# Where modulation tiles, weight splits and start-up transfers stand in a two-block transformer kernel

## The chip, the core and the metric

The kernel runs on one core of a Trainium2 chip. The metric is device microseconds (us) of one execution. The core has a matrix engine (TensorE, called PE in the profile; its weight loads are PEld), a vector engine (DVE), a scalar engine (ACT), GpSimd (POOL), and SyncE (SP), which issues DMAs. SBUF is on-chip memory of 128 partitions; PSUM holds eight banks that PE writes.

## What is computed

Two stacks of depth 2 run one after the other on 256 tokens of width 1024, in fp32. The first has an input projection, three kinds of sequence mixing (a gated recurrence, sparse attention with compressed, selected and windowed keys, and a forgetting attention), an output projection and a squared-ReLU feed-forward. The second is modulated by a condition `c` and carries a second sequence `ctx` of 256 tokens through most of its first layer:

```python
for layer in range(2):
    h = rmsnorm(x, norm1_g[layer]);  proj = h @ w_in[layer]
    mix = concat(hgrn2(...), nsa(...), fox(...))
    x = x + mix @ w_o[layer]
    x = x + square(relu(rmsnorm(x, norm2_g[layer]) @ w_up[layer])) @ w_down[layer]
for l in range(2):
    mod  = silu(c) @ w_ada[l] + b_ada[l]          # 9 vectors of 1024: shifts, scales, gates
    modc = silu(c_ctx) @ w_ada[l] + b_ada[l]
    h  = h  + 0.5 * gt1 * swiglu(ada_norm(h, g_ffn1[l], sh1, sc1), ...)
    ...                                           # conv, latent attention, Fourier branches
    h  = h  + 0.5 * gt3 * swiglu(ada_norm(h, g_ffn2[l], sh3, sc3), ...)
out = rms_norm(h, g_final)
```

## The kernel before

**Weights stream through one ring.** `ring` has 4 slots of 128 x 1024 fp32 (512 KB). SP walks a fixed list of chunks in order (`stream_plan`, `segments`); chunk number n goes into slot n modulo 4, and SP waits until the chunk that lay there has been released (`used[slot]`) before it issues the load. Since SP issues in order, a slot that is released late holds up all loads behind it.

**Split products.** A precise fp32 product is made of three fast ones. For each weight chunk ACT copies the ring slot into `w_hi` (a rounded copy, L733), DVE subtracts it into `w_lo` (L761), both with two buffers, and PE runs the low pass (L802) and then pairs of high passes (L809, L812). ACT may write a `w_hi` only once PE has begun the chunk before, which says that the buffer's old chunk is finished. `splits_ahead` puts the splits of a group's later chunks, and of the next group's first, at the group's start on ACT and DVE; `first_split` does the first chunk of a product.

**The feed-forward of the second block.** `ffn1` and `ffn2` are 22 groups of two chunks (256 or 512 columns; 512 in layer 0, and in layer 1 for `ffn1`). `ffn1_out` and `ffn2_out` are 8 groups of three chunks (8, 8 and 6 tiles of 128). After each of these groups DVE adds the gated result to the residual (L2040) and accumulates squares for the next norm (L1700, L1702), in `gated_add`.

**Where the modulation is computed.** The two layers' modulation is 144 row tiles of 512 KB. 84 of them are done by PE in block 1, as `ada` chunks between its other work: `ADA_TICKS` says how many chunks start at each of 28 points ("ticks") of a layer, ticks 0 to 3 before the attention and ticks 4 to 27 one in each turn of the attention's loop, which runs 22 units through PE, DVE and ACT. `ada_pe` (L883) is this work; a batch of 28 chunks ends with a copy on ACT (L894), 8 small matmuls (L871) and bias adds on DVE (L904). The other 60 are done by DVE in layer 0 of block 2, for layer 1: such a tile comes through the ring as one more chunk of a group, and `row_dot` makes two weighted sums of it (L915 and L917) and releases the slot. `ffn1` and `ffn2` carry one row tile a group; `ffn1_out` carries two a group, taken by `row_pair` at the group's end; `ffn2_out` carries none.

**End of the attention.** ACT copies the last head outputs (L1199), rounds the mixed heads to `hn_hi` (L1390, three parts), DVE makes `hn_lo` (L1395), and then the out-projection `wo` begins with its first split (L733 and L761).

**Start.** ACT issues both halves of `x` (L2578, L2579) and three constant and parameter transfers, then waits for `x`, issues two more (L2585, L2586), waits for the parameters and computes silu of the condition (L2589). PE waits for that before its first matmuls, the mean square (L980). SP issues the first two weight chunks at once.

## Time and profile before

| | us |
|---|---|
| median of 3 runs | 3090.91 (3089.37 to 3092.67) |
| the profiled execution's own time | 3086.55 |
| its span, first to last instruction | 3084.8 |
| PE busy | 2898.1, 94% |
| DVE busy | 1657.1, 54% |
| ACT busy | 1116.2, 36% |
| mean granted clock, share of full | 0.978 |

1.75 us of the profiled execution lie outside the span. Groups of rows further down come from one execution: "idle before" is the time in which an engine waited, with the work that ended the wait behind the arrow; a chain row says what the execution's end was waiting for at that time. "PEclk" is the granted TensorE clock, 1.0 being full.

### The profile page before, as it was taken

What the parts mean: (1) busy time and instruction counts of PE and PEld (TensorE: products, weight loads), DVE (VectorE), ACT (ScalarE), POOL (GpSimd) and SP (SyncE); (2) the same over time, 40 slices, a digit from 0 to 9 for tenths busy, and PEclk for the clock granted to TensorE, in tenths of its full rate; (3) what the DMA queues carried; (4) which work ended last, traced back from release to release, by engine and by line L of the source; (5) the groups of instructions that cost most, each with busy time, mean ns of one, the idle gap of its engine ahead of it and who ended that gap; (6) DMA issues with size and microseconds to landing.
All of it is one profiled execution on the core that took longest, in us unless ns stands there. A gap on an engine that the chain in (4) does not pass through costs nothing.

```text
span 3084.8 us, 45320 instructions
## 1 busy us (share of the span) xinstructions
PE 2898.1 (94%) x16648; PEld 2392.7 (78%) x16648; DVE 1657.1 (54%) x2831; ACT 1116.2 (36%) x1695; POOL 45.8 (1%) x36
## 2 busy tenths in 40 slices
PE   7898998899999998889999999999999998999998
PEld 6658998559988886666566678888788887688998
DVE  6446656346556664469334466653433336645665
ACT  4334535245442221133455232221322223385443
POOL 0100000000000000011000000000000000000000
PEclk9999999899999999999999999999999998999999
DMA  5464554555543443331222224442222223234454
GB/s 185 154 236 151 177 180 135 186 202 194 170 157 132 148 147 117 118 101 38 78 69 62 80 89 146 143 142 94 89 98 95 92 96 100 73 113 142 160 180 144
DMA packets 120091, 401.99 MB, mean 130 GB/s; under 512 B 13088, under 2 KB 22688, under 8 KB 119584
## 3 DMA queue, kind: packets, MB, share of 16 engines
q1 hardware_dynamic: 116320, 392.74, 38.5%
q10 hardware_dynamic: 3648, 7.59, 0.7%
q8 instruction: 79, 1.29, 0.2%
q14 instruction: 44, 0.36, 0.0%
HBM read 399.24 MB, written 1.05 MB: 130 GB/s over the span
## 4 chain that ended last, share of the span: by engine, by line
PE 81%; DVE 10%; DMA 3%; ACT 3%; DVEq 2%; issue 1%; SPq 0%; ACTq 0%
PE bank L802 21%; PE bank L812 21%; PE bank L809 21%; PE bank L2194 4%; DMA ring<-weights 3%; DVE hid L2447 2%; DVE w_lo L761 2%; PE bank L1484 2%; PE bank L883 1%; ACT w_hi L733 1%; PE bank L1942 1%; PE bank L1922 1%; PE bank L2280 1%; DVEq L2453 1%; DVE work L2011 1%
## 5 line engine op out<-in xcount | busy, mean ns | idle before, releaser
L761 DVE TENSOR_TENSOR w_lo<-ring,w_hi 128x1024 fp32r<-128x1024 f32 (+1 forms) x538 | 650.4, 1209 | 915.1 <-ACT w_hi L733 912.3
L733 ACT ACTIVATE w_hi<-ring 128x1024 fp32r<-128x1024 f32 (+1 forms) x538 | 562.9, 1046 | 1388.4 <-PE bank L802 1217.4
L809 PE MATMUL bank<-hn_hi,w_hi 128*128 128x256 f32 (+1 forms) x2816 | 888.3, 335 | 0.0
L812 PE MATMUL bank<-hn_lo,w_hi 128*128 128x256 f32 (+1 forms) x2816 | 887.9, 335 | 0.0
L802 PE MATMUL bank<-hn_hi,w_lo 128*128 128x256 f32 (+1 forms) x2816 | 559.9, 341 | 31.3 <-DVE w_lo L761 20.8
L809 PEld LDWEIGHTS bank<-hn_hi,w_hi 128*128 128x128 f32 x2816 | 539.3, 191 | 52.3
L812 PEld LDWEIGHTS bank<-hn_lo,w_hi 128*128 128x128 f32 x2816 | 539.1, 191 | 52.1
L802 PEld LDWEIGHTS bank<-hn_hi,w_lo 128*128 128x128 f32 x2816 | 444.8, 191 | 101.7 <-issue 45.2
L809 PE MATMUL bank<-hid_hi,w_hi 128*128 128x512 f32 (+1 forms) x704 | 250.3, 365 | 0.0
L812 PE MATMUL bank<-hid_lo_a,w_hi 128*128 128x512 f32 (+1 forms) x640 | 227.2, 364 | 0.0
L802 PE MATMUL bank<-hid_hi,w_lo 128*128 128x512 f32 (+1 forms) x704 | 166.9, 379 | 33.1 <-DVE w_lo L761 28.3
L802 PEld LDWEIGHTS bank<-hid_hi,w_lo 128*128 128x128 f32 x704 | 124.9, 195 | 63.0 <-DVE w_lo L761 35.6
L809 PEld LDWEIGHTS bank<-hid_hi,w_hi 128*128 128x128 f32 x704 | 134.3, 191 | 21.5
L812 PEld LDWEIGHTS bank<-hid_lo_a,w_hi 128*128 128x128 f32 x640 | 121.8, 190 | 19.3
L809 PE MATMUL bank<-up_hi,w_hi 128*128 128x256 f32 x512 | 125.6, 283 | 0.0
L812 PE MATMUL bank<-up_lo,w_hi 128*128 128x256 f32 x512 | 125.6, 283 | 0.0
L2194 PE MATMUL bank<-hid,ring 128*128 128x512 f32 (+1 forms) x352 | 124.2, 494 | 1.3 <-ACT hid L1986 1.3
L2447 DVE SCALAR_TENSOR_TENSOR hid<-work,par,hid 128x512 f32<-128x512 f32 (+1 forms) x180 | 117.4, 707 | 4.6
L812 PEld LDWEIGHTS bank<-up_lo,w_hi 128*128 128x128 f32 x512 | 98.3, 192 | 0.0
L809 PEld LDWEIGHTS bank<-up_hi,w_hi 128*128 128x128 f32 x512 | 98.3, 192 | 0.0
L2194 PEld LDWEIGHTS bank<-hid,ring 128*128 128x128 f32 x352 | 63.8, 189 | 42.7 <-issue 38.8
L1423 PE MATMUL bank<-hn_hi,w_lo 128*128 128x256 f32 (+1 forms) x160 | 58.2, 381 | 28.7 <-ACT hn_hi L971 20.2
(311 smaller groups left out, 3052.7 us busy)
## 6 DMA issues: line engine op xcount, KB each, us to landing
ring<-weights SPq DMA_DIRECT2D x692, 512.0 KB, 3.4
ring<-weights SPq DMA_DIRECT2D x32, 384.0 KB, 3.0
ring<-weights SPq DMA_DIRECT2D x32, 256.0 KB, 2.6
ring<-weights SPq DMA_DIRECT2D x32, 192.0 KB, 2.3
con<-consts ACTq DMA_DIRECT2D x1, 2063.0 KB, 9.1
ring<-weights SPq DMA_DIRECT2D x16, 128.0 KB, 2.1
con<-consts ACTq DMA_DIRECT2D x1, 1088.0 KB, 5.1
res<-x_cm ACTq DMA_DIRECT2D x2, 512.0 KB, 7.7
```

The lines of the kernel that those rows point to most:

```text
L733: act.activation(w_hi[:, even, 0:w], ring[:, slot, 0:w], ACT.Copy).then_inc(s.w_hi, 1)
L761: eng.tensor_tensor(w_lo[:, even, 0:w], ring[:, slot, 0:w], w_hi[:, even, 0:w].bitcast(F32), ALU.subtract).then_inc(s.w_lo, 1)
L802: mm = pe.matmul(dst, w_lo[:, number % 2, k * P:(k + 1) * P], x_hi(k), start=(start and k == order[0]), stop=False)
L809: pe.matmul(dst, high, x_hi(k), start=False, stop=False)
L812: mm = pe.matmul(dst, high, x_lo(k), start=False, stop=(stop and k == order[-1]))
L883: mm = pe.matmul(ada_bank(h)[rows, :], cs[:, k, COND_AT - 2 * q:COND_W - 2 * q], ring[:, slot, i * 4 * P:(i + 1) * 4 * P], start=(q == 0 a ...
L1423: mm = pe.matmul(dst[c], w_lo[:, even[c], k * P:(k + 1) * P], hn_hi[:, k, 0:w], start=(k == 0), stop=False)
L1484: mm = pe.matmul(bank[2 * parity(lin, g)][:, q], sq[:, k, q], ring[:, slot_of(lin, g, 0), k * P:(k + 1) * P], start=(k == 0), stop=(k == K ...
L1922: mm = pe.matmul(scores(x)[:, j * x.keys:(j + 1) * x.keys], q2[0:QK, x.h + j, x.tt * P:(x.tt + 1) * P], k2[0:QK, x.h + j, x.key0:x.key0 + ...
L1942: mm = pe.matmul(bank[7][rows, 0:P], v2[:, x.key0 // P + k, h * DH:(h + 1) * DH], pt[:, x.u % 2, (j * kt + k) * P:(j * kt + k + 1) * P], s ...
L2194: mm = pe.matmul(bank[2 * parity(lin, g)][:, 0:w], ring[:, slot_of(lin, g, 0), k * P:(k + 1) * P], src[:, k, 0:w], start=(k == 0), stop=(k ...
L2447: last = dve.scalar_tensor_tensor(out=dst, in0=src, scalar=taps[:, m, k:k + 1], in1=dst, op0=ALU.mult, op1=ALU.add)
```

## The change

- `ffn1_out` and `ffn2_out` of layer 0 carry **one** row tile a group each, instead of two and none. DVE takes it between the low parts of the group (`split_and_row`), not at its end. A group of either is now four chunks. The last gates' bias and factor 0.5 move to a small `row_gate` in layer 1.
- `ADA_TICKS` becomes a table for each layer: six ticks of two chunks, then ticks of four; 40 chunks in layer 0 and 44 in layer 1, where both had 42. Batches are 20, 20, 24 and 20 chunks instead of three of 28.
- `wo`'s first split moves on ACT from behind the attention into its turn 21, and on DVE ahead of the two last `mix_low`.
- At the start SP issues the first half of `x` ahead of the weights, whose first chunk waits until it has landed; ACT issues four transfers and the two large ones only after the first norm; PE waits for one constant set alone; silu of the condition is made later from a sigmoid (ACT) and a product (DVE).

```diff
-ADA_TICKS = [2, 2, 2, 4, 4, 0, 4, 0, 0, 4, 0, 0, 4, 0, 0, 4, 0, 0, 4, 0, 0, 4, 0, 0, 4, 0, 0, 0]
+ADA_TICKS = ([2, 2, 2, 2, 2, 2, 0, 4, 0, 0, 4, 0, 0, 4, 0, 4, 0, 4, 0, 4, 0, 4, 0, 0, 0, 0, 0, 0],
+             [2, 2, 2, 2, 2, 2, 0, 4, 0, 0, 4, 0, 0, 4, 0, 4, 0, 4, 0, 4, 0, 4, 0, 4, 0, 0, 0, 0])
-ADA_BATCH = 7
+ADA_QUADS = (5, 5, 6, 5)
...
-        order += [("ffn1", l, FF2, (8, 8) + rows, (0, 1)), ("ffn1_out", l, 8, (8, 8, 6) + 2 * rows, (0, 1, 2)),
+        order += [("ffn1", l, FF2, (8, 8) + rows, (0, 1)), ("ffn1_out", l, 8, (8, 8, 6) + rows, (0, 1, 2)),
...
-                  ("ffn2_out", l, 8, (8, 8, 6), (0, 1, 2))]
+                  ("ffn2_out", l, 8, (8, 8, 6) + rows, (0, 1, 2))]
...
                 if n >= 2:
                     unit_out(act, units[n - 2])
                 ada_act(act, l, TICK_ATT + n)
+                if n == len(units) - 1:
+                    first_split(split_high, act, PLAN["wo", l])
...
             mix_high(act, l, 2)
-            first_split(split_high, act, PLAN["wo", l])
...
             attention_dve(dve, l, units_block1(l))
+            first_split(split_low, dve, PLAN["wo", l])
             mix_low(dve, l, 1)
             mix_low(dve, l, 2)
-            first_split(split_low, dve, PLAN["wo", l])
...
             for g in turns(dve, lin, tail=2):
-                split_following(dve, lin, g, following)
+                if lin.cpg > lin.own:
+                    split_and_row(dve, l, which, lin, g, following)
+                else:
+                    split_following(dve, lin, g, following)
                 wait_products(dve, lin, g)
...
-                row_pair(dve, l, lin, g)
...
+        def split_and_row(dve, l, which, lin, g, following):
+
+            at = ROWS_AT["ffn1_out" if which == 0 else "ffn2_out"]
+            to = mods[:, 1, 2 * at:2 * (at + KT)].rearrange("p (m c) -> p m c", c=2)
+            split_ahead(split_low, dve, lin, g, 1, following)
+            row_dot(dve, lin, g, 3, to[:, g.m, :])
+            for j in (2, 3):
+                split_ahead(split_low, dve, lin, g, j, following)
...
+            if which == 0 and l == 1:
+                row_gate(dve, l)
...
             norm_act(act, 2 * l, PLAN["in_t", l], PLAN["down", l - 1] if l else None)
             if l == 0:
+                act.dma_start(con12[:, 0:CONST_SETS[1][1]], consts[1]).then_inc(s.consts1, 16)
+                act.dma_start(res[:, :, T:2 * T], ctx_cm).then_inc(s.ctx_in, 16)
...
         @block.sync
         def _(sp):
+            sp.dma_start(res[:, 0:KT // 2, 0:T], x_cm[:, 0:KT // 2, :]).then_inc(s.x_in, 16)
...
+                        if isinstance(chunk, int) and chunk == 0:
+                            sp.wait_ge(s.x_in, 16)
...
         @block.tensor
         def _(pe):
-            pe.wait_ge(s.consts, 48)
-            pe.wait_ge(s.csilu, 1)
+            pe.wait_ge(s.con0_in, 16)
...
         @block.scalar
         def _(act):
-            act.dma_start(res[:, 0:KT // 2, 0:T], x_cm[:, 0:KT // 2, :]).then_inc(s.x_in, 16)
             act.dma_start(res[:, KT // 2:KT, 0:T], x_cm[:, KT // 2:KT, :]).then_inc(s.x_in2, 16)
-            act.dma_start(con0[:, :], consts[0]).then_inc(s.consts, 16)
+            act.dma_start(con0[:, :], consts[0]).then_inc(s.con0_in, 16)
+            act.dma_start(par12[:, 0:PARAM_SETS[1][1]], params[1]).then_inc(s.consts, 16)
             act.dma_start(par0[:, :], params[0]).then_inc(s.consts, 16)
```

DVE's queue in the first groups of `ffn1_out`, layer 0, before. L761 makes a low part, L915 and L917 are one row tile, L2040, L1700 and L1702 are the gated add and the squares:

```order
L761 TENSOR_TENSOR w_lo<-ring,w_hi 128x1024 [waits w_hi]
L761 TENSOR_TENSOR w_lo<-ring,w_hi 128x768 [waits w_hi]
L761 TENSOR_TENSOR w_lo<-ring,w_hi 128x1024 [waits w_hi]
L2040 SCALAR_TENSOR_TENSOR res<-bank,mods,res 128x256 [waits used2]
L2040 SCALAR_TENSOR_TENSOR res<-bank,mods,res 128x256
L1700 TENSOR_TENSOR work<-res 128x512
L1702 TENSOR_TENSOR work<-work 128x512
L915 SCALAR_TENSOR_TENSOR conds,mods<-ring,con_65 128x1024 [waits landed3]
L917 SCALAR_TENSOR_TENSOR ring,mods<-ring,con_65 128x1024
L915 SCALAR_TENSOR_TENSOR conds,mods<-ring,con_65 128x1024 [waits landed0]
L917 SCALAR_TENSOR_TENSOR ring,mods<-ring,con_65 128x1024
L761 TENSOR_TENSOR w_lo<-ring,w_hi 128x1024 [waits w_hi]
```

The same engine and product after the change (the seventh group; the loop that runs the first six has the same order; L765 is L761, L923 and L925 are L915 and L917, L2071 is L2040):

```order
L765 TENSOR_TENSOR w_lo<-ring,w_hi 128x1024 [waits w_hi]
L923 SCALAR_TENSOR_TENSOR conds,mods<-ring,con_65 128x1024 [waits landed3]
L925 SCALAR_TENSOR_TENSOR ring,mods<-ring,con_65 128x1024
L765 TENSOR_TENSOR w_lo<-ring,w_hi 128x768 [waits w_hi]
L765 TENSOR_TENSOR w_lo<-ring,w_hi 128x1024 [waits w_hi]
L2071 SCALAR_TENSOR_TENSOR res<-bank,mods,res 128x256 [waits used2]
L2071 SCALAR_TENSOR_TENSOR res<-bank,mods,res 128x256
L1729 TENSOR_TENSOR work<-res 128x512
L1731 TENSOR_TENSOR work<-work 128x512
L765 TENSOR_TENSOR w_lo<-ring,w_hi 128x1024 [waits w_hi]
```

Four row instructions between the squares and the next low part have become two behind that low part. The group's row tile is always in slot 3 now.

ACT's queue at the end of the attention of layer 0, after the change (L737 is L733, L1209 copies a unit's transposed weights, L1216 is L1199, L1416 is L1390):

```order
L1216 ACTIVATE work<-bank 128x128 [waits att_v]
L737 ACTIVATE w_hi<-ring 128x1024 [waits lo_used,landed1]
L1209 ACTIVATE work<-bank 128x512 [waits att_v,att_t]
L1216 ACTIVATE work<-bank 128x128 [waits att_v]
L1416 ACTIVATE hn_hi<-work 128x4x256 [waits att_o]
L1216 ACTIVATE work<-bank 128x128 [waits att_v]
L1416 ACTIVATE hn_hi<-work 128x2x256 [waits att_o]
L737 ACTIVATE w_hi<-ring 128x1024 [waits lo_used,landed2]
```

The first `L737` stood between the last `L1416` and the second `L737` before. On DVE the low part of the same chunk has moved ahead of the two `hn_lo` subtractions in the same way.

## Rows read from the trace of the kernel before

**Rows 1.** The page: busy time of each engine, and the chain's shares.
```profile
PE 2898.1 (94%) x16648; PEld 2392.7 (78%) x16648; DVE 1657.1 (54%) x2831; ACT 1116.2 (36%) x1695; POOL 45.8 (1%) x36
...
PE 81%; DVE 10%; DMA 3%; ACT 3%; DVEq 2%; issue 1%; SPq 0%; ACTq 0%
```

**Rows 2.** `ffn1_out`, `ffn2_out`: length; PE, PEld, DVE, ACT, POOL busy; clock; DMA share.
```profile
1165.03:1335.57 170.54, 136.13 (x536) 106.15 (x537) 85.76 (x128) 28.65 (x33) 1.53 (x1) 0.93 0.37 123
2072.77:2198.00 125.23, 122.20 (x537) 100.37 (x537) 49.30 (x70) 28.85 (x33) 0.00 (x0) 1.00 0.32 101
```

**Rows 3.** Chain of waits in `ffn1_out`, layer 0: start, length, what.
```profile
1176.39 3.33 DMA ring<-weights
...
1180.83 1.22 DVE w_lo L761
...
1184.50 1.23 DVE conds L915
1185.73 1.14 DVE ring L917 x2
1186.97 1.23 DVE conds L915 x2
1188.20 1.15 DVE ring L917 x2
1189.35 1.15 DVE w_lo L761
```

**Rows 4.** DVE in one group of `ffn2_out`, layer 0: start, length.
```profile
2088.03 0.88 DVE L2040 SCALAR_TENSOR_TENSOR res<-bank,mods,res 128x256 f32<-128x256 f32 x2 [1.48 <-PE bank L812]
...
2090.37 1.22 DVE L761 TENSOR_TENSOR w_lo<-ring,w_hi 128x1024 fp32r<-128x1024 f32 x1
2094.63 0.96 DVE L761 TENSOR_TENSOR w_lo<-ring,w_hi 128x768 fp32r<-128x768 f32 x1 [3.04 <-ACT w_hi L733]
2100.29 1.23 DVE L761 TENSOR_TENSOR w_lo<-ring,w_hi 128x1024 fp32r<-128x1024 f32 x1 [4.70 <-ACT w_hi L733]
```

**Rows 5.** Stretches: `ffn1` with a row tile a group (layer 0), without (layer 1).
```profile
920.84:1165.03 244.19, 241.83 (x1057) 199.10 (x1057) 153.02 (x224) 64.80 (x81) 0.00 (x0) 0.99 0.40 138
2198.00:2442.15 244.15, 241.62 (x1056) 199.02 (x1057) 100.77 (x136) 62.99 (x80) 0.00 (x0) 0.99 0.28 92
```

**Rows 6.** The start on DVE and PE, in order of time.
```profile
7.33 1.43 DVE L2613 TENSOR_TENSOR work<-res 128x256 f32<-128x256 f32 x4 [4.66 <-DMA res<-x_cm]
10.12 1.43 DVE L2613 TENSOR_TENSOR work<-res 128x256 f32<-128x256 f32 x4 [1.36 <-DMA res<-x_cm]
...
12.87 5.48 PE L980 MATMUL bank<-work,con 128*128 128x256 f32 x16 [12.87 <-ACT conds L2589]
...
20.46 0.36 PE L1423 MATMUL bank<-hn_hi,w_lo 128*128 128x256 f32 x1 [2.11 <-ACT hn_hi L964]
```

**Rows 7.** PE: first two products of `wo`, layer 0; first, layer 1.
```profile
243.11 2.05 PE L802 MATMUL bank<-hn_hi,w_lo 128*128 128x256 f32 x8 [3.28 <-issue]
248.37 1.23 PE L802 MATMUL bank<-hn_hi,w_lo 128*128 128x256 f32 x8
...
688.82 2.05 PE L802 MATMUL bank<-hn_hi,w_lo 128*128 128x256 f32 x8 [3.28 <-issue]
```

**Rows 8.** Modulation chunks on PE around the start of layer 0's attention.
```profile
154.72 3.68 PE L883 MATMUL bank<-ring,conds 128*32 128x512 f32 x12 [0.54 <-DMA ring<-weights]
...
173.24 1.70 PE L883 MATMUL bank<-ring,conds 128*32 128x512 f32 x4 [1.55 <-DMA ring<-weights]
...
180.74 1.92 PE L883 MATMUL bank<-ring,conds 128*32 128x512 f32 x16
```

**Rows 9.** Chain in layer 0's attention: the fourth load of a four.
```profile
192.23 7.41 DMA ring<-weights
```

**Rows 10.** The last batch in layer 1's attention, on PE.
```profile
679.59 1.06 PE L871 MATMUL bank<-con,work 128*128 128x14 f32 x8 [0.86 <-ACT work L894]
```

**Rows 11.** All waits of PE in looped product `down`, layer 0 (373:463).
```profile
PE bank L802 <- DVE w_lo L761: 1.1, 1, 1.1
```

More of the change, by code:

```diff
@@ L100 @@
 LOW_AFTER_TAP = {0: 1, 3: 2, 6: 3, 9: 4, 10: 5, 11: 6, 12: 7, 13: 8, 14: 9}
-ADA_TICKS = [2, 2, 2, 4, 4, 0, 4, 0, 0, 4, 0, 0, 4, 0, 0, 4, 0, 0, 4, 0, 0, 4, 0, 0, 4, 0, 0, 0]
-ADA_CHUNKS = sum(ADA_TICKS)
-ADA_UPTO = list(itertools.accumulate(ADA_TICKS))
+ADA_TICKS = ([2, 2, 2, 2, 2, 2, 0, 4, 0, 0, 4, 0, 0, 4, 0, 4, 0, 4, 0, 4, 0, 4, 0, 0, 0, 0, 0, 0],
+             [2, 2, 2, 2, 2, 2, 0, 4, 0, 0, 4, 0, 0, 4, 0, 4, 0, 4, 0, 4, 0, 4, 0, 4, 0, 0, 0, 0])
+ADA_CHUNKS = tuple(sum(t) for t in ADA_TICKS)
+ADA_UPTO = [list(itertools.accumulate(t)) for t in ADA_TICKS]
 TICK_EARLY, TICK_ATT = 0, 4
-ADA_BATCH = 7
-ADA_BATCHES = DEPTH * ADA_CHUNKS // (4 * ADA_BATCH)
-COND_AT = 2 * ADA_BATCH - 2
+ADA_QUADS = (5, 5, 6, 5)
+ADA_FROM = [0] + list(itertools.accumulate(ADA_QUADS))
+ADA_WIDEST = max(ADA_QUADS)
+assert 4 * ADA_FROM[2] == ADA_CHUNKS[0] and 4 * ADA_FROM[4] == sum(ADA_CHUNKS)
+COND_AT = 2 * ADA_WIDEST - 2
 COND_W = COND_AT + COL_GROUP
 ROW_TILES = 72
-ROWS_AT = {"ffn1": DEPTH * ADA_CHUNKS - ROW_TILES}
+ROWS_AT = {"ffn1": sum(ADA_CHUNKS) - ROW_TILES}
 ROWS_AT["ffn1_out"] = ROWS_AT["ffn1"] + FF2
-ROWS_AT["ffn2"] = ROWS_AT["ffn1_out"] + 2 * KT
-assert ROWS_AT["ffn2"] + FF2 == ROW_TILES
+ROWS_AT["ffn2"] = ROWS_AT["ffn1_out"] + KT
+ROWS_AT["ffn2_out"] = ROWS_AT["ffn2"] + FF2
+assert ROWS_AT["ffn2_out"] + KT == ROW_TILES
 def stream_plan():
@@ L130, in stream_plan @@
                   ("mix_out", l, 8, (8,), (0,)), ("ffn2", l, FF2, (8, 8) + rows, (0, 1)),
-                  ("ffn2_out", l, 8, (8, 8, 6), (0, 1, 2))]
+                  ("ffn2_out", l, 8, (8, 8, 6) + rows, (0, 1, 2))]
     for name, l, n, tiles, split in order:
-        own = {"ffn1": 2, "ffn1_out": 3, "ffn2": 2}.get(name, len(tiles))
+        own = {"ffn1": 2, "ffn1_out": 3, "ffn2": 2, "ffn2_out": 3}.get(name, len(tiles))
         plan[name, l] = Product(chunk, group, n, tiles, split, split0, own)
@@ L387, in feed_forward @@
                 put(t[:, c:c + 8])
-            if l == 0 and name == "ffn1":
-                put(rows[ROWS_AT["ffn1_out"] + 2 * m])
-                put(rows[ROWS_AT["ffn1_out"] + 2 * m + 1])
+            if l == 0:
+                put(rows[ROWS_AT[f"{name}_out"] + m])
     for l in range(DEPTH):
@@ L856, in ada_chunk @@
         def ada_chunk(m):
-            chunk = PLAN["ada", m // ADA_CHUNKS].chunk + m % ADA_CHUNKS
+            l = int(m >= ADA_CHUNKS[0])
+            chunk = PLAN["ada", l].chunk + m - ADA_CHUNKS[0] * l
             return chunk % SLOTS, chunk // SLOTS
         def ada_started(l, t):
-            return range(ADA_CHUNKS * l + (ADA_UPTO[t - 1] if t else 0), ADA_CHUNKS * l + ADA_UPTO[t])
+            first = ADA_CHUNKS[0] * l
+            return range(first + (ADA_UPTO[l][t - 1] if t else 0), first + ADA_UPTO[l][t])
         def ada_done(l, t):
-            return [h for h in range(ADA_BATCHES) if t >= 0 and 4 * ADA_BATCH * (h + 1) - 1 in ada_started(l, t)]
+            return [h for h in range(len(ADA_QUADS)) if t >= 0 and 4 * ADA_FROM[h + 1] - 1 in ada_started(l, t)]
         def ada_pe(pe, l, t):
@@ L889, in ada_act @@
             for h in ada_done(l, t - 1):
-                slot, turn = ada_chunk(4 * ADA_BATCH * (h + 1) - 1)
+                slot, turn = ada_chunk(4 * ADA_FROM[h + 1] - 1)
                 act.wait_ge(used[slot], turn + 1)
@@ L918, in row_dot, with row_bias, row_gate @@
                                      op0=ALU.mult, op1=ALU.mult, accum_out=to[:, 1:2]).then_inc(used[slot], 1)
-        def row_bias(dve, l):
-            to = mods[:, l, 2 * ROWS_FIRST:2 * ROW_TILES].rearrange("p (m c) -> p m c", c=2)
-            bias = param("bada")[:, 72 * l + ROWS_FIRST:72 * (l + 1)]
-            dve.tensor_tensor(to, to, bias.unsqueeze(2).broadcast_to([P, ROW_TILES - ROWS_FIRST, 2]), ALU.add)
+        def row_bias(dve, l, first, last):
+            to = mods[:, l, 2 * first:2 * last].rearrange("p (m c) -> p m c", c=2)
+            bias = param("bada")[:, 72 * l + first:72 * l + last]
+            dve.tensor_tensor(to, to, bias.unsqueeze(2).broadcast_to([P, last - first, 2]), ALU.add)
+        def row_gate(dve, l):
+            dve.drain()
+            row_bias(dve, l, ROWS_AT["ffn2_out"], ROW_TILES)
+            dve.drain()
+            gate_rows = mods[:, l, 2 * ROWS_AT["ffn2_out"]:2 * ROW_TILES]
+            dve.tensor_scalar(gate_rows, gate_rows, 0.5, None, ALU.mult)
         SHIFT, SCALE, GATE = (0, 3, 6), (1, 4, 7), (2, 5, 8)
@@ L1371, in hg_act @@
                 act.drain()
+                if l == 0:
+                    act.wait_ge(s.consts, 32)
+                    act.activation(krot[:, 0:2 * KT], param("cvec"), ACT.Sigmoid).then_inc(s.csig, 1)
                 act.activation(sg, proj_b[:, 0:2 * T], ACT.Sigmoid)
@@ L2137, in ffn_dve @@
                         row_dot(dve, lin, g, 2, to[:, g.m, :])
+            if which == 0 and l == 1:
+                row_gate(dve, l)
             if which == 2 and l < DEPTH - 1:
                 dve.drain()
-                row_bias(dve, l + 1)
+                row_bias(dve, l + 1, ROWS_AT["ffn1"], ROWS_AT["ffn2_out"])
                 gates_dve(dve, l + 1)
```

63 lines of the change are left out of this document (29 added, 34 removed).

## The prediction

> **What bounds the kernel now.** I read the page first: PE is busy 94% of the span and 81% of the chain of waits is PE's own work, DVE 10%, DMA and ACT 3% each [rows 1]. The change takes no matmul away. It can win only where PE stands idle or runs at a low clock because it stood idle. So I next looked at stretches in which PE's work takes longer than the same work elsewhere. Four places came out: `ffn1_out` of layer 0, the start, the head of `wo`, and the attention with its modulation chunks.
>
> **`ffn1_out`, layer 0, two row tiles down to one.** It and `ffn2_out` are the same 536 or 537 matmuls, and take 170.54 and 125.23 us, at a granted clock of 0.93 and 1.00; PE is busy 136.13 and 122.20 us [rows 2]. The row tiles are the difference: DVE is busy 85.76 against 49.30. The chain shows how 45.3 us are lost in eight groups, 5.7 each [rows 3]. A group ends; DVE does its gated add, its squares and then four row instructions (1.23, 1.14, 1.23, 1.15), and only then the low part (1.15) that PE waits for. The last row instruction also frees the ring slot, so the load of the next chunk is issued late and the group after waits for it (3.33 of the chain) before the splits even begin.
>
> The order after the change has one tile behind the group's second low part. Does it fit there? A group takes 125.23 / 8 = 15.65 us with everything in; from the rows of one group its steady length is 15.0 and PE starts its chunks at about 0, 5.4 and 10.9 us of it. DVE is done with the gated add and squares and begins the low part of the second chunk 2.4 us after the group's start (2087.8) and ends it at 3.8 [rows 4]. It is then free until 6.8 (idle 3.04) and again for 4.70 before the fourth low part [rows 4]. A row tile is 1.23 + 1.15 = 2.4 us of DVE. If it has landed by 4.4 it ends at 6.8, just when the third chunk's rounded copy is there; if it is later, the third low part (0.96) may slip until 9.9 before PE, which wants it at 10.9, sees anything. So about 3 us are spare, and the 4.70 behind it hold the rest. I take the cost as nothing. The nearest rows on that: `ffn1` takes 244.19 us with a row tile a group and 244.15 without, though DVE is busy 153.02 against 100.77 [rows 5]. What is then late next is nothing on DVE: 8 tiles more or less, DVE stays under half busy.
>
> `ffn1_out` falls to what `ffn2_out` is: **-45.3**. `ffn2_out` gains a tile a group under the same sum: **0**. Bounds, both together: a small leak of 0.5 us a group gives -37; none at all with its last norm a little earlier gives -47. The gates' bias and half (`row_gate`, two or three small instructions on DVE) stand before `ffn1_out` of layer 1, where DVE has such gaps too: 0.
>
> **Loops.** With equal groups these two products become loops where PE and DVE ran through written-out groups. `down` is such a loop, and within it PE waits just once, 1.1 us, for a low part [rows 11]. I take the way back of a loop at 0. The Trainium skill, "Runtime: NRT & Kernel Launch", section "Instruction fetch mechanics", says otherwise: a taken branch whose target lies outside the fetched window has to wait for a DMA that fetches it, which is why kernels prefer unrolling. By it the two loops would cost a fetch at each way back (a rival, below).
>
> **Start.** The squares of the two halves of `x` begin at 7.33 and 10.12, PE's mean square at 12.87 (it waits for silu of the condition), takes 5.48, and the first product begins at 20.46 [rows 6]. So from PE's 12.87 to the first product are 7.6 us, of which nothing shrinks. After the change `x` has the DMA engines nearly to itself (1 MB and the constants, where 1 MB of weights lay beside it), and silu is off the path. The squares then follow the data: from the last half's squares, 10.12 + 1.43 = 11.55, to an earlier end. I estimate the halves' landing at 5.5 to 6 instead of 7.3 and 10.1, since half the bytes are in front of them, so the last square ends near 7.3, and PE can start near 6.5 with its first half and is done near 12.0 instead of 18.35. The weights now begin after the first half has landed, near 5.9. A load alone takes 3.33 [rows 3], these two share the engines with the second half of `x`, so I put their landing near 9.5 and 10.9, and the second one's copy and subtraction (1.06 + 1.23) near 13.2. That is what is last then, by a little: the norm comes near 13.2 and the first product near 14.4. That is **-6**; if the weights come at once, -7.3; if they land 2 us later, -4. Sigmoid and product that replace silu add some **+0.3**. The large transfers (second constants, context) go out behind the first norm, some 6 us later than before, and are wanted first by work near 30 us; with 9 to 10 us to land they are in time by about 3.
>
> **Head of `wo`.** PE stands for 3.28 us before `wo`'s first product, in each layer (ends at 243.11 and at 688.82), and then that product is slow: 2.05 us for its eight low matmuls against 1.23 for the next ones, and 5.26 us from the first product to the second [rows 7]. The gap is ACT's copy and DVE's low part, about 1.06 + 1.23, behind the last copies. Both are made earlier now, in the attention's last turn. What is late next is the rounded head outputs' third part, 0.8 to 1 us after PE's last attention matmul. PE keeps 2.3 to 3.3 us a layer and some of the slow product: **-4** a layer, **-8** for both. The copy put into ACT's last turn costs 1.06 us of ACT there, about 0.2 of it on the path. Bounds -6.5 and -8.3.
>
> **Modulation.** The chunks before layer 0's attention are paced by DMA: twelve matmuls take 3.68 us and still wait 0.54 [rows 8], where sixteen take 1.92 at full speed [rows 8]; a four at the attention's third turn waits 1.55 [rows 8]. The table now puts 8 instead of 10 chunks before the attention and gives two more turns twos, so loads have more time: by hand, tick by tick against these rates, layer 0 gains 8 to 9 us up to the fourth turn. Later the fours stand two turns apart, some 6.6 us, instead of three. The fourth load of a four took 7.41 us from its issue [rows 9], so a four two turns behind another finds its last chunk about 1.5 us late, four times in layer 0 and five in layer 1: some of that comes back. In layer 1 the last batch is folded two turns earlier or at the end where it costs its small matmuls (1.06) and a wait of 0.86 [rows 10]; one batch more costs the like again. I take **-6** for layer 0, **-2** for layer 1, **-8** together. From both sides: if all the later stalls are paid in full and no early ones saved, +4; if none come, -14.
>
> **The sum.** -45.3 - 6 + 0.3 - 8 - 8 = -67. The profiled execution took 3086.55 and would take 3019.5. The median of the runs before is 4.4 above that profiled one, so on their base I forecast 3090.9 - 67 = **3024**.
>
> **Rivals.**
> *A row tile between the low parts still holds PE.* Each group then loses a wait like the 1.1 in `down` [rows 11] or up to 1.5 us, in all 16 groups of both products, 18 to 24 us: 3042 to 3048. For it: DVE must wait for the tile's landing, and the third low part stands behind. Against it: [rows 5], and the 3 us to spare.
> *The fours two turns apart give the modulation's gain back.* DMA moves the same bytes in fewer turns; 7.41 [rows 9] may be the rule when the ring's other loads share it. The term is 0 to +4 instead of -8: 3032 to 3036.
> *The loops pay a fetch.* PE's waits at three or so more ways back in each of two loops, each as long as a short load, 2 to 3.3 us [rows 3], would add 8 to 13: 3032 to 3037. Against it: [rows 11]. The Trainium skill's section on instruction fetch speaks for it, and this loop's trace doesn't agree with it.
> *Slower.* The row tile lands so late that DVE, which takes its queue in order, stands before it while the third low part is due. The landing may be 6.7 us behind the issue before anything is lost (row tile needed by 7.3 of the group, issued at 0.6), and each us after that costs 1 us in each of 16 groups. A fourth load took 7.41 [rows 9]. To turn 67 us round, it must lose 4.2 us a group, so land 11 us after its issue, twice what the 3.33 of [rows 3] and the DMA share of 0.32 [rows 2] let expect. It would give over 3091.
> *The change doesn't do what it says* in part: if the start's path goes over a wait that I don't see (the weights behind `x`), -6 becomes 0, 3030. That is inside the forecast's own range.
>
> **Chances and numbers.** The forecast has 0.74, with a range of its own of 3014 to 3034, from the bounds of the small terms taken half together. The held row tile has 0.11, the modulation 0.08, the loops 0.05, slower 0.02. To leave out no more than 2 in 10, the range goes from 3012 (start -7, modulation -14, norm a little earlier) to 3043. A measurement of this kernel tells about 0.2%, 6 us. All cases but the last lie more than 40 us below the kernel before: faster 0.96, within 0.2% 0.02, slower 0.02.
>
> **What would show it.** The stretch from the first matmul of `ffn1_out` to that of the next norm at 125 us, clock 1.00, with no wait of PE for a low part; above 130 the row tiles leak. `ffn2_out` at 125.2, with DVE some 19 us busier; if it is longer and the wait is on a low part behind the row, the second rival is true; if the wait is on fetching or "issue" at equal distances, the loops. PE's first matmul near 6.5 and the first product near 14.4. The gap before `wo` at most 1 us and its first product at 1.2 us for eight. In the attention, waits on the ring's loads in turns where fours stand two apart: up to 1.5 us each as forecast, more if the modulation's gain is lost. The forecast is wrong if `ffn1_out` stays above 140 us: its 45 us are two thirds of the whole.

## The result

| | before | after |
|---|---|---|
| time, median of 4 runs | 3091.26 (3089.37 to 3092.67) | 3037.93 (3035.34 to 3043.71) |
| ratio | | 0.9833, 95% interval 0.9821 to 0.9846 |
| span of the profiled execution | 3084.8 | 3033.2 |
| PE busy | 2898.1 | 2884.0 |
| mean granted clock | 0.978 | 0.984 |

The kernel is 53 us faster (53 in this measurement of it, 49 in a second one, below). The forecast was 3024, its range 3012 to 3043, its own likeliest case 3014 to 3034. The measured time lies in the range and not in that case: 14 us of the gain are missing, and it lies above the second rival's 3032 to 3036 too.

The first lines of the page after, to be read against [rows 1]: the matmuls are all there (eight more belong to the fourth batch), DVE has the same work, and PE's share of the chain has risen by what DVE's has lost.

```profile
PE 2884.0 (95%) x16656; PEld 2385.5 (79%) x16656; DVE 1657.1 (55%) x2837; ACT 1115.0 (37%) x1695; POOL 45.8 (2%) x36
...
PE 83%; DVE 8%; DMA 3%; ACT 2%; DVEq 2%; issue 1%; SPq 0%; ACTq 0%
```

`ffn1_out` and `ffn2_out` of layer 0 after, as in [rows 2] (length; PE, PEld, DVE, ACT, POOL busy; clock; DMA share). The first has lost 45.3 us and equals the second, which has taken on 18.4 us of DVE work for nothing:

```profile
1159.50:1284.72 125.22, 122.19 (x536) 100.39 (x537) 66.91 (x96) 28.90 (x33) 1.53 (x1) 1.00 0.39 134
2022.36:2147.59 125.23, 122.21 (x536) 100.40 (x537) 67.74 (x101) 28.89 (x33) 0.00 (x0) 1.00 0.40 134
```

DVE in one group of `ffn1_out` after, the counterpart of [rows 4]. The low part at 1192.21 stands before the tile; DVE waits 0.93 for the tile's landing, and the tile is done at 1196.7:

```profile
1189.86 0.88 DVE L2071 SCALAR_TENSOR_TENSOR res<-bank,mods,res 128x256 f32 x2 [1.69 <-PE bank L816]
1190.83 0.69 DVE L1729 TENSOR_TENSOR work<-res 128x512 f32 x1
1191.60 0.69 DVE L1731 TENSOR_TENSOR work<-work 128x512 f32<-128x512 f32 x1
1192.21 1.22 DVE L765 TENSOR_TENSOR w_lo<-ring,w_hi 128x1024 fp32r<-128x1024 f32 x1
1194.36 1.23 DVE L923 SCALAR_TENSOR_TENSOR conds<-ring,con 128x1024 f32<-128x1024 f32 x1 [0.93 <-DMA ring<-weights]
```

In the stretch from there to the next norm PE waits for no low part at all. What PE waits for between 1160 and 1290 us:

```profile
PE bank L1449 <- ACT hn_hi L988: 2.6, 1, 2.6
PE bank L1005 <- DVE work L1736: 0.4, 2, 0.2
```

**Where the difference lies, from one trace to the other.** At the first product the changed kernel is 4.5 us ahead; at the first modulation chunk of layer 0 (146.44 before, 144.74 after) 1.7; at `wo`'s first product of layer 0 3.4; at that of layer 1 5.1; at the norm behind `ffn1_out` 50.9; at the end 51.6. So one product holds seven eighths of it, and start, heads of `wo` and modulation, from which the forecast expected 22 us, gave 5.5 together up to `ffn1_out` (1165.03 to 1159.50).

### The profile page after: what moved, and what is told of

Its sections match the earlier page's. It is cut to its first block, busy times and chain, and to the rows that moved or that the text cites. A ratio compares the mean times of both kernels' runs of the same rounds, so it can differ in the third digit from the quotient of the medians.

```text
span 3033.2 us, 45608 instructions
## 1 busy us (share of the span) xinstructions
PE 2884.0 (95%) x16656; PEld 2385.5 (79%) x16656; DVE 1657.1 (55%) x2837; ACT 1115.0 (37%) x1695; POOL 45.8 (2%) x36
## 3 DMA queue, kind: packets, MB, share of 16 engines
q8 instruction: 76, 1.25, 0.2%
HBM read 399.24 MB, written 1.05 MB: 132 GB/s over the span
## 4 chain that ended last, share of the span: by engine, by line
PE 83%; DVE 8%; DMA 3%; ACT 2%; DVEq 2%; issue 1%; SPq 0%; ACTq 0%
PE bank L806 22%; PE bank L816 22%; PE bank L813 22%; PE bank L2226 4%; DMA ring<-weights 3%; DVE hid L2479 2%; PE bank L1510 2%; DVE w_lo L765 2%; PE bank L1971 1%; PE bank L1951 1%; DVEq L2485 1%; DVE hn_lo L1013 1%; PE bank L2312 1%; DVE work L2040 1%; ACT w_hi L737 1%
## 5 line engine op out<-in xcount | busy, mean ns | idle before, releaser
L765 DVE TENSOR_TENSOR w_lo<-ring,w_hi 128x1024 fp32r<-128x1024 f32 (+1 forms) x538 | 650.4, 1209 | 844.4 <-ACT w_hi L737 842.0
L737 ACT ACTIVATE w_hi<-ring 128x1024 fp32r<-128x1024 f32 (+1 forms) x538 | 563.0, 1047 | 1347.6 <-PE bank L806 1255.1
L806 PE MATMUL bank<-hn_hi,w_lo 128*128 128x256 f32 (+1 forms) x2816 | 559.9, 342 | 25.3 <-DVE w_lo L765 21.2
L806 PEld LDWEIGHTS bank<-hn_hi,w_lo 128*128 128x128 f32 x2816 | 444.2, 191 | 96.6 <-issue 40.6
L806 PE MATMUL bank<-hid_hi,w_lo 128*128 128x512 f32 (+1 forms) x704 | 157.5, 364 | 7.9 <-DVE work L2152 4.9
L923 DVE SCALAR_TENSOR_TENSOR conds<-ring,con 128x1024 f32<-128x1024 f32 x60 | 73.5, 1226 | 25.8 <-DMA ring<-weights 14.5
```

The lines of the kernel that those rows point to most:

```text
L737: act.activation(w_hi[:, even, 0:w], ring[:, slot, 0:w], ACT.Copy).then_inc(s.w_hi, 1)
L765: eng.tensor_tensor(w_lo[:, even, 0:w], ring[:, slot, 0:w], w_hi[:, even, 0:w].bitcast(F32), ALU.subtract).then_inc(s.w_lo, 1)
L806: mm = pe.matmul(dst, w_lo[:, number % 2, k * P:(k + 1) * P], x_hi(k), start=(start and k == order[0]), stop=False)
L923: dve.scalar_tensor_tensor(out=conds[:, :], in0=ring[:, slot, :], scalar=1.0, in1=crow[:, 0:D], op0=ALU.mult, op1=ALU.mult, accum_out=to[: ...
```

## The experiments

Each kernel is compared with the kernel before, run beside it on the same chip; the difference of the medians is given in brackets. The chunk matmuls (L883 before, L893 after) are one group in a view by lines, whose busy time and idle time together I call chunk time below; "attention with modulation" is the stretch from the first modulation chunk of a layer to the first matmul of its `wo`, summed over both layers.

**The row tiles' part alone, on the kernel before.** The edit is the part of the change that concerns row tiles, nothing else:

```diff
-("ffn1_out", l, 8, (8, 8, 6) + 2 * rows, (0, 1, 2))
+("ffn1_out", l, 8, (8, 8, 6) + rows, (0, 1, 2))
-("ffn2_out", l, 8, (8, 8, 6), (0, 1, 2))
+("ffn2_out", l, 8, (8, 8, 6) + rows, (0, 1, 2))
...
-                split_following(dve, lin, g, following)
+                if lin.cpg > lin.own:
+                    split_and_row(dve, l, which, lin, g, following)
+                else:
+                    split_following(dve, lin, g, following)
```

> The kernel before with the row tiles' part alone: one a group in ffn1_out and ffn2_out of layer 0, between the low parts, and the gates' small step. Theory: the whole of its gain is ffn1_out's stretch, 170.5 to about 125.5 us, ffn2_out stays at 125.2, so 45 us faster than before, span near 3040. Rival (other parts freed DMA and DVE for it, or its loops cost something in ffn2_out): less than 40.

Measured: 3045.04 against 3090.43 (-45.4), ratio 0.9852 (0.9835 to 0.9868). Its two out-products:

```profile
1168.62:1293.87 125.25, 122.22 (x536) 100.40 (x537) 66.90 (x96) 28.90 (x33) 1.53 (x1) 1.00 0.39 134
2033.59:2158.83 125.24, 122.21 (x537) 100.37 (x537) 67.60 (x101) 28.91 (x33) 0.00 (x0) 1.00 0.39 134
```

The term of 45.3 is right to the tenth in the trace. In the time the interval of the ratio is 41 to 51 us, so a match to the tenth there is chance. All that the other parts bring together is then 53.3 - 45.4 = 8 us, less in the second measurement of the changed kernel.

**One row tile a group, at the group's end.**

```diff
             for g in turns(dve, lin, tail=2):
-                if lin.cpg > lin.own:
-                    split_and_row(dve, l, which, lin, g, following)
-                else:
-                    split_following(dve, lin, g, following)
+                split_following(dve, lin, g, following)
...
                 square(dve, g.m, 0, w_next).then_inc(s.squares, 1)
+                row_one(dve, which, lin, g)
```

> The changed kernel with its one row tile a group at the group's end, behind the squares, in both out-products. It tells the number of tiles from their place. By the rows of a group DVE's low part of the second chunk would end at about 2.5 + 2.4 + 1.2 = 6.1 us of a group and PE wants it at 5.4: 0.7 us a group and a little more, 131 to 135 us for each product instead of 125, some 10 to 18 us slower than the changed kernel. Rival (two tiles a group were the whole trouble, one is hidden anywhere): no change.

Measured: 3065.21 against 3090.43 (-25.2), ratio 0.9916 (0.9899 to 0.9932), some 25 us slower than the changed kernel. Each product takes 12 us more, at a PE that is busy only 2.2 us more:

```profile
1165.96:1303.08 137.12, 124.43 (x537) 99.83 (x537) 67.46 (x96) 28.89 (x33) 1.53 (x1) 0.99 0.36 122
2042.66:2180.29 137.63, 124.37 (x536) 99.83 (x537) 68.15 (x101) 28.88 (x33) 0.00 (x0) 0.99 0.36 122
```

PE's waits there (2042 to 2180 us: in total, how often, the longest) name the low part, once in every group but the first:

```profile
PE bank L806 <- DVE w_lo L765: 8.1, 7, 1.5
```

So place matters as well as number, and the expected 10 to 18 us were too few. With one tile at the end a group's cost is about 1.5 us, with two (before) 5.7, with one behind the second low part nothing. My 0.7 us a group was too small by half. In the group of `ffn1_out` that PE begins at 1197.49 the tile begins 3.2 us into the group, not 2.5; the low part ends at 6.7, and PE has stood since 5.6. PE's wait is 8.1 / 7 = 1.2 where it occurs, 1.0 over eight groups. PE's own 2.2 us more are another 0.3 a group; the last 0.2 to 0.3 I can't name.

**The out-projection's first split put back behind the attention.**

```diff
-                if n == len(units) - 1:
-                    first_split(split_high, act, PLAN["wo", l])
...
             mix_high(act, l, 2)
+            first_split(split_high, act, PLAN["wo", l])
...
-            first_split(split_low, dve, PLAN["wo", l])
             mix_low(dve, l, 1)
             mix_low(dve, l, 2)
+            first_split(split_low, dve, PLAN["wo", l])
```

> The changed kernel with the out-projection's first split back behind the attention on ACT and DVE. Forecast's theory: the 3.28 us gap before each first product comes back, and some of the slow first product: 4 us a layer, 8 us slower, span near 3041. Rival (the gap only moves, since the rounded heads end the wait anyway): 2 us or less in both layers together.

Measured: 3044.40 against 3090.43 (-46.0), ratio 0.9854 (0.9837 to 0.987): 3 to 7 us slower than the changed kernel (its two measurements stand at -53.3 and -48.7), where 8 was expected. The interval overlaps the changed kernel's two, so the time alone doesn't show the loss; the trace does. The gap is back with the same 3.28. First PE's first two products of `wo` in this kernel, then the same in the changed kernel, with the last attention matmuls ahead of them:

```profile
242.96 2.05 PE L806 MATMUL bank<-hn_hi,w_lo 128*128 128x256 f32 x8 [3.28 <-issue]
247.26 1.12 PE L806 MATMUL bank<-hn_hi,w_lo 128*128 128x256 f32 x8
```

```profile
239.08 0.66 PE L1106 MATMUL bank<-work 128*64 128x128 f32 x8 [0.66 <-ACT work L1216]
239.67 1.61 PE L806 MATMUL bank<-hn_hi,w_lo 128*128 128x256 f32 x8
243.90 1.19 PE L806 MATMUL bank<-hn_hi,w_lo 128*128 128x256 f32 x8 [0.71 <-DVE w_lo L765]
```

From the attention's last matmul to the second product are 4.16 us in the changed kernel (239.74 to 243.90), 7.6 with the split put back, 8.54 before. In layer 1 they are 3.9, 7.6 and 7.8. The clock was part of it: before, that stretch had a mean granted clock of 0.61 of full, so it ran mostly at the lower of the two levels (1.2 and 2.4 GHz), with a PE that had stood for 3.28 us; after, 1.00, the upper level throughout. The two stretches, before and then after:

```profile
239.83:248.37 8.54, 5.26 (x25) 5.29 (x25) 4.71 (x5) 2.94 (x5) 0.00 (x0) 0.61 0.14 58
```

```profile
239.74:243.90 4.16, 3.35 (x24) 2.97 (x25) 3.68 (x5) 1.90 (x4) 0.00 (x0) 1.00 0.02 4
```

**The modulation part undone alone.** The changed kernel with the table and the three batches of before:

```diff
-ADA_TICKS = ([2, 2, 2, 2, 2, 2, 0, 4, 0, 0, 4, 0, 0, 4, 0, 4, 0, 4, 0, 4, 0, 4, 0, 0, 0, 0, 0, 0],
-             [2, 2, 2, 2, 2, 2, 0, 4, 0, 0, 4, 0, 0, 4, 0, 4, 0, 4, 0, 4, 0, 4, 0, 4, 0, 0, 0, 0])
+ADA_TICKS = ([2, 2, 2, 4, 4, 0, 4, 0, 0, 4, 0, 0, 4, 0, 0, 4, 0, 0, 4, 0, 0, 4, 0, 0, 4, 0, 0, 0],) * 2
-ADA_QUADS = (5, 5, 6, 5)
+ADA_QUADS = (7, 7, 7)
```

> The changed kernel with the table and the three batches of 28 chunks of the kernel before: the modulation part undone alone. Forecast: the new table and batches save 8 us, so this is 8 us slower than the changed kernel, 3046 to 3049. Revised: chunk time is 71.4 us on average over five profiles of the changed table and 67.7 over two of the old one, and the attention's other time is 120.5 against some 117; undoing it saves 3 to 7 us: 3031 to 3036, chunk time 67 to 69, the rest near 117. Rival (the table neither wins nor loses): 3037 to 3041.

Measured: 3030.53 (3029.26 to 3033.65, 5 runs) against 3091.75 (-61.2), ratio 0.98 (0.9785 to 0.9814). That interval ends below the changed kernel's two (0.9821 to 0.9846, and 0.9822 to 0.986 again). The modulation's new table and batches cost 8 to 12 us, where the forecast had them save 8. Its median is also the lowest of all kernels here, by 0.9 us, which is no difference.

**What in the table costs it.** Six kernels vary spacing and batches, and one repeats the changed kernel. Only the one with the modulation undone, above, has an interval clear of both of the changed kernel's; differences of a few us among the rest are hints.

The changed kernel again:

> The changed kernel itself once more, for how far its stretches and its time repeat, and beside the next two on one chip. Its code up to the fold of modulation batches was run in other experiments: first product at 14.7 to 16.0, the stretches with modulation and attention 92 to 98 us (layer 0) and 93 to 96 (layer 1). Expected: time 3035 to 3040, no stretch outside these.

Measured: 3040.93 against 3089.64 (-48.7), ratio 0.9841 (0.9822 to 0.986). It fell just outside what was expected, in the time and in both stretches (98.8 and 97.4).

Spaced as before, 40 and 44 chunks, four batches (`[2, 2, 2, 4, 4, 0, 4, 0, 0, 4, ...]`, the last of layer 0 a two, the third of layer 1 a four):

> The changed kernel with a table that is spaced as before: fours from the fourth tick on, later fours three turns apart, still 40 and 44 chunks in four batches. Forecast's theory (the new spacing saves about 8 us): this is 8 us slower than the changed kernel, span near 3041. Revised theory (what the early twos save is paid back by the fours two turns apart; the waits of chunks add up to 68 us in both traces): within 2 us of the changed kernel, span 3031 to 3035.

Measured: 3037.89 against 3090.75 (-52.9), ratio 0.9826 (0.98 to 0.9851). The old spacing alone brings nothing back, as the revised theory said.

The six twos kept, and later fours three turns apart where they fit:

```diff
-ADA_TICKS = ([2, 2, 2, 2, 2, 2, 0, 4, 0, 0, 4, 0, 0, 4, 0, 4, 0, 4, 0, 4, 0, 4, 0, 0, 0, 0, 0, 0],
-             [2, 2, 2, 2, 2, 2, 0, 4, 0, 0, 4, 0, 0, 4, 0, 4, 0, 4, 0, 4, 0, 4, 0, 4, 0, 0, 0, 0])
+ADA_TICKS = ([2, 2, 2, 2, 2, 2, 0, 4, 0, 0, 4, 0, 0, 4, 0, 0, 4, 0, 0, 4, 0, 0, 4, 0, 0, 4, 0, 0],
+             [2, 2, 2, 2, 2, 2, 0, 4, 0, 0, 4, 0, 4, 0, 0, 4, 0, 0, 4, 0, 4, 0, 0, 4, 0, 4, 0, 0])
```

> The changed kernel with its six early twos kept, and the fours three turns apart where there is room (all seven in layer 0; in layer 1 five of seven steps are three or two mixed). Revised theory: the second four of a pair, which took 4.2 to 5.2 us in the changed kernel where a lone one took 1.85 to 3, becomes cheap; chunk time falls from 68.9 to near 60, span about 3025. Rival (the low sum of a stretch is set by the loads' pace as such, not by the spacing): no change, 3033.

Measured: 3036.29 against 3090.75 (-54.5), ratio 0.9825 (0.9798 to 0.9851), and a chunk time of 69.0: not the 60 of the theory, but about what the rival said.

The changed table with one batch a layer (`ADA_QUADS = (10, 11)`):

> The changed kernel with the same table of chunks, but batches of 40 and 44 chunks: two folds instead of four. Revised theory: each fold costs PE its 0.96 us of small matmuls and a wait of about 1.7 us for DVE behind it, so two fewer save about 5 us, span near 3028. Rival (DVE's lateness in that turn has another cause and the fold is hidden): 1 us or less, span 3032 to 3034.

Measured: 3033.14 against 3090.75 (-57.6), ratio 0.9813 (0.9788 to 0.9838).

With six batches (`ADA_QUADS = (3, 3, 4, 4, 4, 3)`):

> The changed kernel with the same table and batches of 12, 12, 16, 16, 16 and 12 chunks: six folds instead of four, so that folds have three points (two, four, six). Theory: each fold costs 2.4 us or more, 5 to 8 us slower than the changed kernel, 3042 to 3046. Rival (one batch a layer was faster for another reason, a bank or the place of the last fold): within 2 us of the changed kernel.

Measured: 3038.67 against 3089.64 (-51.0), no slower than four, as the rival said.

One batch a layer and wide spacing (layer 1 with eight twos, then fours three turns apart but for the last):

> The changed kernel with batches of 40 and 44 chunks and a table in which a four comes three turns behind the last (once two in layer 1, which has eight twos first). If the two causes add up: 6 to 8 us faster than the changed kernel in the profile, span 3021 to 3026, chunk time near 60 to 64 us. Rival (spacing is worth nothing beyond the batches): as the one with one batch a layer alone, 3023 to 3028 with chunk time near 67.

Measured: 3031.42 against 3090.43 (-59.0), ratio 0.9806 (0.9789 to 0.9823), with a chunk time of 67.1, the rival's.

Seven twos and seven fours, all three turns apart, in both layers, two batches:

> The changed kernel with 42 chunks in each layer, seven twos and then seven fours, all three turns apart, and two folds in all. No pair of fours two turns apart is left. Theory: as the wide spacing with one batch a layer (3031.4) or 1 to 2 us faster, 3029 to 3032; 6 to 8 us faster than the changed kernel on the same chip. Rival: spacing is worth nothing, and the two chunks more in layer 0's busy early turns cost it: 3033 to 3036.

Measured: 3036.20 against 3089.64 (-53.4). That is 4.7 faster than the changed kernel on the same chip and no faster than its first measurement, close above the rival's 3033 to 3036 and not the 3029 to 3032 of the theory.

What their traces show, in us:

| kernel | batches | chunk time | attention with modulation | time against before |
|---|---|---|---|---|
| before; row part alone | 3 | 69.4; 69.0 | 191.8; 190.2 | 0; -45.4 |
| changed; again | 4 | 70.5; 76.5 | 190.2; 196.3 | -53.3; -48.7 |
| changed table, start staggered | 4 | 67.7 | 185.7 | -51.6 |
| changed table, row tile at end | 4 | 75.7 | 194.4 | -25.2 |
| changed table, `wo`'s split back | 4 | 74.9 | 199.4 | -46.0 |
| modulation undone | 3 | 69.5 | 183.3 | -61.2 |
| spaced as before | 4 | 72.3 | 192.1 | -52.9 |
| twos, then threes | 4 | 69.0 | 187.6 | -54.5 |
| changed table | 2 | 68.3 | 181.7 | -57.6 |
| changed table | 6 | 67.2 | 187.3 | -51.0 |
| wide spacing | 2 | 67.1 | 180.9 | -59.0 |
| sevens | 2 | 66.1 | 183.9 | -53.4 |

Chunk time is the sum of the two numbers behind the bar in such a row (busy, mean ns, idle before). Here those of the changed kernel, of the same kernel again, and of the one with the modulation undone:

```profile
L893 PE MATMUL bank<-ring,conds 128*32 128x512 f32 x336 | 59.2, 612 | 11.3 <-DMA ring<-weights 11.2
```

```profile
L893 PE MATMUL bank<-ring,conds 128*32 128x512 f32 x336 | 65.8, 650 | 10.7 <-DMA ring<-weights 10.4
```

```profile
L893 PE MATMUL bank<-ring,conds 128*32 128x512 f32 x336 | 60.8, 646 | 8.7 <-DMA ring<-weights 8.5
```

Three things follow. First, with the changed table and four batches the attention takes 185.7 to 199.4 us, and the two gaps of 3.28 lie in it where `wo`'s split stands behind it. Without these gaps it is 191.9 on average in the five profiles with the changed table and four batches, and 184.1 (183.3 to 185.2) in the three with the old table and three batches: 7.8 more. Of these, 3.8 are chunk time, and 4.0 are the rest of the stretch. That rest goes with the number of batches better than chunk time does: 113.8 to 115.8 with three, 118.0 to 119.8 with four, 120.1 with six, 113.4 and 113.8 with two; but 117.8 in the sevens, which also have two.

Second, fours two turns apart do run slower, as the second rival said. In the changed kernel's layer 0 the fours of turns 11 and 15 take 1.21 + 1.26 + 1.05 + 0.17 + 1.05 = 4.7 and 4.4 us, while a lone one runs in 1.92:

```profile
185.41 1.93 PE L893 MATMUL bank<-ring,conds 128*32 128x512 f32 x16
191.23 1.21 PE L893 MATMUL bank<-ring,conds 128*32 128x512 f32 x8
193.70 1.05 PE L893 MATMUL bank<-ring,conds 128*32 128x512 f32 x4 [1.26 <-DMA ring<-weights]
194.93 1.05 PE L893 MATMUL bank<-ring,conds 128*32 128x512 f32 x4 [0.17 <-DMA ring<-weights]
199.67 2.19 PE L893 MATMUL bank<-ring,conds 128*32 128x512 f32 x16
```

With the modulation undone, the same stretch of time has them three turns apart, at 1.9 to 3.0:

```profile
180.17 1.92 PE L893 MATMUL bank<-ring,conds 128*32 128x512 f32 x16
188.28 2.77 PE L893 MATMUL bank<-ring,conds 128*32 128x512 f32 x16
197.04 1.92 PE L893 MATMUL bank<-ring,conds 128*32 128x512 f32 x16
207.42 2.97 PE L893 MATMUL bank<-ring,conds 128*32 128x512 f32 x16
```

What the early turns save doesn't cover it: over the five profiles with the changed table and four batches, chunk time is 67.7 to 76.5, mean 73.1, against 69.3 in three of the old one. But the spacing isn't shown to be the cause of the lost time: put back alone, with four batches kept, it left the time where it was (-52.9).

Third, batches count, but not one by one. In layer 0 of the changed kernel PE waits 4.2 us for DVE, with one batch a layer 2.1; 0.6 of either is elsewhere, the rest stands behind the folds (1.7 and 1.8 behind two, 1.5 behind one). PE's waits in layer 0's attention with modulation, changed and then one batch a layer:

```profile
PE bank L893 <- DMA ring<-weights: 4.8, 9, 1.3
PE bank L1087 <- DVE work L1175: 4.2, 3, 1.8
```

```profile
PE bank L893 <- DMA ring<-weights: 3.6, 7, 1.3
PE bank L1087 <- DVE work L1175: 2.1, 2, 1.5
```

One fold more thus costs its 0.96 of matmuls and 2.1 of waiting there. But six folds were no slower than four, and in them that wait is 2.1 again in layer 0. So what a fold costs depends on the turn it falls in, and my price per fold fell with the six batches. How the 8 to 12 us part between spacing, folds and the two chunks that moved from layer 0 to layer 1 stays open: with the spacing alone, layer 0's stretch is 91.0 against 92.2 to 98.8 but layer 1's is 96.6 against 93.5 to 97.4, and the time 1 to 6 us less; with one batch a layer alone the time is 4 to 9 us less; and both together gain no more than going back. The kernel spaced as before and the one with the modulation undone differ only in four batches against three and in 40 and 44 chunks against 42 and 42, and the second was 8 us faster, their intervals just overlapping. The changed table with three batches, which would part them further, is not among the runs.

**Start staggered.** The third load waits for the second's landing:

```diff
                         if isinstance(chunk, int) and chunk == 2:
-                            sp.wait_ge(s.x_in2, 16)
+                            sp.wait_ge(landed[1], 16)
```

> The changed kernel; the third weight load at the start waits until the second has landed. In the changed kernel all four loads go out within 1.4 us, share the DMA engines, and the first two land at 11.4 and 12.7, which with their copies holds the first norm. Theory: they land near 9.5 and 10.5, the first product starts near 14.9 instead of 16.0, 1 us saved. Rival (the constants' transfers set the pace): the first product stays at 16.0; or the third and fourth loads come late and PE waits for them later, nothing saved.

Measured: 3039.15 against 3090.75 (-51.6). The loads land at 10.8 and 12.0, and the first product starts at 15.55. All three lie within what the eleven unstaggered kernels show (9.8 to 11.4, 11.0 to 12.7, 14.5 to 16.0). So no effect of the other two loads on the first two is seen, and one profile couldn't show one below the 1.6 us of that spread.

## Why the prediction was right, and where it was not

**Row tiles: right, by its steps.** -45.3 forecast, -45.3 in the trace and -45.4 in time measured alone. It is seven eighths of the gain in the trace, and what kept the forecast within its range. The tile landed 3.8 us behind its issue, DVE waited 0.93 for it and was done with it about 3 us before the next low part had to begin, as much as forecast. The first rival (a wait of 1 to 1.5 us a group) and the slower one (a late landing) didn't happen between the low parts; the first is exactly what happens when the tile stands at the group's end, 12 us a product.

One reading there was wrong and did no harm: DVE doesn't stay under half busy in such a product, it is at 53% (66.91 of 125.22).

**Loops: right.** `ffn2_out` is a loop now and takes 125.23, as written out; no wait at its ways back appears. It has five of them, not three, so the rival was also priced too low. The Trainium skill ("Runtime: NRT & Kernel Launch", section "Instruction fetch mechanics") says that a taken branch has to wait for a fetch where its target lies outside the two pages held. Whether the start of a turn lies outside them here no run shows, so these loops neither bear the rule out nor speak against it.

**Head of `wo`: right in the trace.** -4.4 in layer 0 (8.54 to 4.16) and -3.9 in layer 1, against -4 each; undone, it cost 3 to 7 us in time, not clear of noise. The first product's eight low matmuls still took 1.61 and 1.60 where 1.2 was forecast, and 2.08 in layer 1 of the changed kernel again. What was late next was not the third part of the rounded heads alone but the second chunk's low part (a wait of 0.71).

**Start: the size right, and partly given back.** PE's first matmuls came at 6.68 (6.5 forecast). The first product was at 16.0 in this trace and 14.5 to 15.7 in ten others with the same start, where 14.4 was forecast; before it stood at 20.46, and 21.08 in the row part alone. What was short is the loads' landing: 11.4 and 12.7 in this trace instead of 9.5 and 10.9, and 9.8 to 11.1 and 11.0 to 12.4 in the ten others. Where they came at 9.9 and 11.2, in the changed kernel again, the first product stood at 14.48, as forecast. The 0.3 for silu no run tells apart. Start on ACT and DVE after, to be held against [rows 6]:

```profile
11.41 1.06 ACT L737 ACTIVATE w_hi<-ring 128x1024 fp32r<-128x1024 f32 x1 [7.11 <-DMA ring<-weights]
12.51 2.52 DVE L765 TENSOR_TENSOR w_lo<-ring,w_hi 128x1024 fp32r<-128x1024 f32 x2 [3.94 <-ACT w_hi L737]
12.71 1.06 ACT L754 ACTIVATE w_hi<-ring 128x1024 fp32r<-128x1024 f32 x1 [0.23 <-DMA ring<-weights]
13.67 0.46 ACT L975 ACTIVATE work<-bank,small 128x256 f32<-128x256 f32 x1
```

From the first product to the first modulation chunk the kernels with the new start need 127.2 to 131.0 us, those with the old one 126.0 and 127.1. So about 2 of 5.5 us are given back before 147 us. In this trace it is 2.7, and half of that lies in one place, where the clock is lower. The same 13 matmuls took 1.66 us before (56.59 to 58.25) and 2.93 after (52.48 to 55.41), at a granted clock of 0.50, the lower level. The ten us around them, 35 us behind the first product, before and then after:

```profile
55.46:65.46 10.00, 9.96 (x95) 9.62 (x96) 5.25 (x9) 4.60 (x7) 0.00 (x0) 1.00 0.42 143
```

```profile
51.01:61.01 10.00, 9.77 (x81) 9.32 (x82) 5.25 (x9) 3.29 (x5) 0.00 (x0) 0.83 0.30 99
```

The changed kernel again has this place too, at 51 to 54 us. PE had been busy 7.7 and 7.9 of the ten us ahead of it, before and after, so why the clock fell in one and not in the other these rows don't tell. The large transfers have landed by 31.6 us, and up to there PE has lost 0.2.

**Modulation: wrong, and this is the step that missed.** The term was -6 and -2 us, and +4 its upper bound; it is +8 to +12 by the experiment that undoes it, above that bound, which was also the top of the second rival's 0 to +4. Three sizes in it were off. All are sums of the chunk rows and the idle time before them, over five profiles with the changed table and four batches and three with the old one.

- The early turns of layer 0 were to gain 8 to 9 us up to the attention's fourth turn. They gained 5: 22.3 us of chunk time became 17.3, and one of these 5 is only that there are two chunks fewer.
- Later in layer 0 the same 24 chunks took 18.5 instead of 13.9, so 4.6 came back and layer 0 kept nothing. I had 1.5 us for each of four late fours. Two were late, each by 2.5 to 4 us more than a lone one, since several of their chunks run at the loads' pace (1.05 + 0.2 us instead of 0.48) and not only the last. Their sum, 5 to 7.5, is near my 6; only "some of that" was to come back.
- Layer 1, forecast at -2, has 37.3 instead of 33.0. I also took a fold's cost at its matmuls, without the wait for DVE behind it: 4.8 us behind the four folds of the changed kernel, 2.8 behind the three of the kernel before.

These sizes show where the time went in the traces. That they are the cause of the whole 8 to 12 us isn't shown: the old spacing alone brought nothing back, one batch a layer 4 to 9 us, not clear of noise.

**Then the sum.** -45.4 for the rows, -8 for `wo`, -4 for the start, +8 for the modulation make -49, where -49 and -53 were measured. Without the modulation's part they make -57, where -61.2 was measured, so it closes to 4 us, as near as the intervals of these times (4 to 5 us to each side) let one ask. Of the missing 14 us the modulation's 16 are more than all, and the start's 2 and these 4 nearly cancel. The range held because its upper end was drawn for a row tile that holds PE, which didn't happen; that it also covered a modulation term of the wrong sign is luck. Its lower end was added up wrongly, without effect: the bounds named for it give 3015, not 3012.

## What to carry to other kernels

A piece of work that is hidden in one place of a queue can cost 1.5 us a group one place earlier, so ask of each piece which instruction behind it PE wants next, and when. Bursts of loads that share one ring are paid at the loads' pace by the engine that consumes them; a chunk then took 1.25 us instead of 0.48, and a table that saved stalls early and bunched later saved nothing in layer 0. Of a change with four parts, undo each alone: here one part took back most of what two others brought, and the total hid it. Where two causes are suspected inside a part, undo each alone too: here the old spacing alone brought back nothing, though the traces showed what the new one costs.
